# One trunk layer on one core: the first two input projections in two halves of the features, and the order of the first weight loads

## The reference

```python
sh1, sc1, g1, sh2, sc2, g2 = split(silu(cond) @ w_ada + b_ada, 6)   # "modulation", 12 blocks of 512 columns
h = ln_plain(x) * (1 + sc1) + sh1                                   # 384 x 1024
q_a, k_a, v_a, q_g, k_g, v_g, r_g, lr, mg = split(h @ w_in, ...)    # "projections"
attn = block_attention(rope(rms(q_a)), rope(rms(k_a)), v_a)
z = lr @ gla_w_gate + gla_b_gate ; logg = log_sigmoid(z) / 16
gla = rms(gla_scan(q_g, k_g, v_g, logg)) * silu(r_g)
merged = sigmoid(mg0) * (attn @ w_br_attn) + sigmoid(mg1) * (gla @ w_br_gla)
x = ln_affine(alpha * x + g1 * (merged @ w_out))
x = ln_affine(alpha * x + g2 * moe(ln_plain(x) * (1 + sc2) + sh2))  # top 2 of 32 experts
```

## Time and profile before

| | |
|---|---|
| median of three runs | 716.77 us |
| the profiled execution | 715.41 us, span 713.7 us |
| TensorE busy | 635.1 us, 89% of the span |
| VectorE, ScalarE, GpSimd busy | 277.9, 109.6, 113.1 us |
| HBM read | 174.55 MB |
| mean granted clock of TensorE | 0.941 |

### The profile page before, as it was taken

The page is one execution under the profiler, slowest core; times in us unless marked ns, Lnnn a source line. Parts: engine busy times, 40 slices in busy tenths (PEclk is TensorE's granted clock), DMA queues, the critical chain, the costliest instruction groups (busy, mean ns, idle before and its releaser), DMA issues.

```text
span 713.7 us, 8198 instructions
## 1 busy us (share of the span) xinstructions
PE 635.1 (89%) x3225; PEld 346.4 (49%) x3225; DVE 277.9 (39%) x568; ACT 109.6 (15%) x227; POOL 113.1 (16%) x115
## 2 busy tenths in 40 slices
PE   2899999999999999999999974899998888888894
PEld 0374345554444455556444453566664544544431
DVE  2421543236745445213224766133333222322247
ACT  0020252220012122215010020211111001100000
POOL 3000000020300000000000221433333222231100
PEclk9679999999999999999999985799999999999998
DMA  9977444236430230308968087599999999999852
GB/s 337 368 247 252 161 182 149 87 118 236 141 119 5 113 118 1 118 3 298 370 246 321 29 296 292 190 406 405 406 405 405 407 404 403 400 403 402 353 214 88
DMA packets 67495, 176.60 MB, mean 247 GB/s; under 512 B 10420, under 2 KB 12500, under 8 KB 67456
## 3 DMA queue, kind: packets, MB, share of 16 engines
q1 hardware_dynamic: 50832, 143.56, 52.8%
q10 hardware_dynamic: 10880, 24.21, 9.6%
q0 software_dynamic: 5744, 8.28, 3.3%
HBM read 174.55 MB, written 11.96 MB: 261 GB/s over the span
## 4 chain that ended last, share of the span: by engine, by line
PE 69%; DMA 15%; DVE 6%; SPq 6%; issue 2%; ACT 1%; POOL 1%; DVEq 0%; POOLq 0%
PE bank L1478 24%; PE bank L1733 10%; DMA X<-exp_w_up 9%; PE bank L1650 6%; PE bank L1664 6%; PE bank L1742 5%; DMA W<-exp_w_up 3%; DMA X<-w_ada 3%; SPq L451 3%; PE bank L1430 2%; PE bank L1608 2%; PE bank L1626 2%; PE bank L1531 1%; PE bank L1719 1%; SPq L461 1%
## 5 line engine op out<-in xcount | busy, mean ns | idle before, releaser
L1478 PE MATMUL bank<-W,Y 128*128 128x512 f32 (+1 forms) x432 | 183.0, 577 | 0.0
L1478 PEld LDWEIGHTS bank<-W,Y 128*128 128x128 f32 x432 | 80.9, 192 | 85.2 <-issue 82.6
L1733 PE MATMUL bank<-X,Y 128*64 128x256 f32 x704 | 86.6, 401 | 11.0 <-DMA X<-exp_w_up 10.2
L1733 PEld LDWEIGHTS bank<-X,Y 128*64 128x64 f32 x704 | 55.7, 145 | 48.0 <-DMA X<-exp_w_up 19.3
L630 POOL TENSOR_TENSOR rstd<-ss,cst 128x1 f32<-128x1 f32 (+3 forms) x21 | 22.6, 1074 | 339.2 <-DVE ss L760 339.2
L673 POOL DMA_INDIRECT Y<-h_rows,gidx x32 | 41.4, 1293 | 105.4 <-PE bank L1719 93.9
L1139 DVE COPY abias<-bank 128x128 f32<-128x128 f32 x32 | 9.3, 291 | 122.0 <-PE bank L1764 122.0
L1733 PE MATMUL bank<-W,Y 128*64 128x256 f32 (+1 forms) x320 | 39.7, 368 | 9.0 <-DMA W<-exp_w_up 4.6
L1742 PE MATMUL bank<-X,abias 128*64 128x512 f32 x176 | 42.6, 602 | 1.8 <-issue 1.8
L678 POOL DMA_INDIRECT pair_rows<-PTr,sidx x32 | 32.5, 1014 | 65.8 <-DVE PTr L1153 59.3
L1650 PE MATMUL bank<-W,Y 128*128 128x512 f32 x96 | 42.0, 594 | 0.3 <-PE bank L1650 0.3
(11 more groups left out here) (224 smaller groups left out, 705.6 us busy)
## 6 DMA issues: line engine op xcount, KB each, us to landing
X<-exp_w_gate SPq DMA_DIRECT2D x22, 1024.0 KB
X<-exp_w_up SPq DMA_DIRECT2D x22, 1024.0 KB
X<-exp_w_down SPq DMA_DIRECT2D x22, 1024.0 KB, 19.2
W<-w_in SPq DMA_DIRECT2D x8, 2048.0 KB, 9.0
Y<-w_ada ACTq DMA_DIRECT2D x8, 2048.0 KB, 9.2
W<-exp_w_gate SPq DMA_DIRECT2D x10, 1024.0 KB
W<-exp_w_up SPq DMA_DIRECT2D x5, 1024.0 KB
W<-exp_w_down SPq DMA_DIRECT2D x5, 1024.0 KB
```

The lines of the kernel that those rows point to most:

```text
L1478: ins = mm(bank[:, 0:cols], hT[:, i, k, :], w[:, k, :], start=k == 0, stop=k == KT - 1)
L1733: ins = mm(bank[hh * 64:hh * 64 + 64, a:b], x_[:, c, h * 64:h * 64 + 64], rhs(hh), start=k == 0 and a == 0, stop=k == KT - 1, skip_group_c ...
```

## The change

`WEIGHTS` loses ("ada", 1). SyncE's queue loads in the order: constants, x, block 0, block 2, the first half (features 0 to 511) of kvl, the first half of gqk, block 1, block 3, the second halves, the small tensors. Block 3 goes to `adabuf`. x is transposed and copied to `hT` by ScalarE as it is; VectorE then scales and shifts `hT` in place, half by half (`modulate(g)`). The two halved projections run their slices 0 to 3 first, for all tiles, and slices 4 to 7 later into the same banks. TensorE starts with 8 products on the constants that nobody reads (`keep_busy`). The step list moves: blocks 4 to 8 now stand behind projections 5 to 9 instead of 1, 3, 5, 7, 9; `lr` 1, `z` 1, `lr` 2 and `z` 2 go one or two projections later.

```diff
-AFTER[4] += [("z", 0), ("lr", 1), ("kprep", 1)]
-AFTER[5] += [("z", 1), ("lr", 2), ("kprep", 2)]
-AFTER[6] += [("kT", 0), ("kT", 1), ("z", 2), ("cum", 0)]
-AFTER[7] += [("kT", 2), ("kT", 3), ("tr", 0), ("cum", 1)]
+AFTER[4] += [("z", 0), ("kprep", 1)]
+AFTER[5] += [("lr", 1), ("kprep", 2)]
+AFTER[6] += [("z", 1), ("lr", 2), ("kT", 0), ("kT", 1), ("cum", 0)]
+AFTER[7] += [("z", 2), ("kT", 2), ("kT", 3), ("tr", 0), ("cum", 1)]
...
-for _n, _j in zip(range(4, 12), (1, 3, 5, 7, 9, 11, 12, 14)):
+for _n, _j in zip(range(4, 12), (5, 6, 7, 8, 9, 11, 12, 14)):
     AFTER[_j + 1].insert(0, ("rows", _n))
     AFTER[_j].insert(0, ("ada", _n))
...
+            def modulate(g):
+                bank = side.wait_full(dve, "modc", g)
+                mc = bank[:, 0:4 * KT].rearrange("p (k s) -> p k s", s=2)
+                ks = slice(4 * g, 4 * g + 4)
+                step(V.tensor_copy(modc[:, ks, :], mc[:, ks, :]))
+                ks = slice(KT + 4 * g, KT + 4 * g + 4)
+                ins = V.tensor_scalar_add(modc[:, ks, :], mc[:, ks, :], 1.0)
+                ...
+                for i in range(TILES):
+                    side.wait_read(dve, "xT", i, g)
+                    for k in range(4 * g, 4 * g + 4):
+                        ins = V.tensor_scalar(hT[:, i, k, :], hT[:, i, k, :], modc[:, KT + k, stream(i):stream(i) + 1],
+                                              modc[:, k, stream(i):stream(i) + 1], ALU.mult, ALU.add)
+                    ins.then_inc(h_ready[g], 1)
+            normed(0)
+            normed(1)
+            modulation(0)
+            normed(2)
+            modulation(2)
+            modulate(0)
+            modulation(1)
+            modulation(3)
+            modulate(1)
...
+            def x_columns(i):                                  # ScalarE
+                for g in range(2):
+                    bank = side.wait_full(act, "xT", i, g)
+                    side.was_read(A_(hT[:, i, 4 * g:4 * g + 4, :].rearrange("p k t -> p (k t)"), bank[:, :], ACT.Copy),
+                                  "xT", i, g)
+            x_columns(0)
+            x_columns(1)
+            main.wait_read(act, "ada", 0)
+            bias_rows(2)
+            x_columns(2)
+            main.wait_read(act, "ada", 1)
+            bias_rows(3)
+            main.wait_read(act, "ada", 2)
+            bias_rows(4)
+            main.wait_full(act, "ada", 3)
             ada_block(4)
...
+            def keep_busy(count):                              # TensorE
+                for _ in range(count):
+                    mm(banks[6][:, :], ident, cst[:, 0:HALF], start=True, stop=True)
...
             pe.wait_ge(S["consts_in"], 16)
+            keep_busy(FILL_START)                              # 8
+            x_transposes(0)
             pe.wait_ge(S["cond_silu"], 2)
+            modulation(0)
+            x_transposes(1)
+            columns(colbank, 0, 0)
+            x_transposes(2)
+            modulation(2)
+            side.filled(columns(colbank, 16, 2), "modc", 0)
+            for i in range(TILES):
+                project_half("kvl", i, 0)
+            modulation(1)
+            project_half("gqk", 0, 0)
+            columns(colbank, 8, 1)
+            modulation(3)
+            project_half("gqk", 1, 0)
+            side.filled(columns(colbank, 24, 3), "modc", 1)
+            project_half("gqk", 2, 0)
```

More of the change, by code:

```diff
@@ L96, in constants @@
     return c
-WEIGHTS = ([("ada", n) for n in range(2)]
+WEIGHTS = ([("ada", 0)]
            + [(x, 0) for x in ("kvl", "gqk", "vg", "q", "rg")] + [("mg", n) for n in range(4)]
@@ L147, with __init__ @@
 STEPS = [x for j in range(len(PROJ)) for x in AFTER[j]]
+FILL_START = 8
 class Banks:
-    def __init__(self, banks, full, read, jobs):
-        self.at = {}
-        uses = {b: 0 for b in range(len(banks))}
+    def __init__(self, ring, banks, full, read, jobs, uses, known=None):
+        self.at = dict(known or {})
         for n, job in enumerate(jobs):
-            b = n % len(banks)
+            b = ring[n % len(ring)]
             self.at[job] = (banks[b], full[b], read[b], uses[b])
@@ L185, in wait_read, with first_jobs @@
         eng.wait_ge(self.at[job][2], self.at[job][3] + 1)
+HALVED = ("kvl", "gqk")
+def first_jobs():
+    jobs = {("modc", g): 7 for g in range(2)}
+    jobs.update({("xT", 0, 0): 0, ("xT", 0, 1): 1, ("xT", 1, 0): 3, ("xT", 1, 1): 0, ("xT", 2, 0): 1, ("xT", 2, 1): 3})
+    jobs.update({("ada", n): 2 for n in (0, 2, 1, 3)})
+    for kind, ring in zip(HALVED, ((4, 5, 6), (0, 1, 3))):
+        jobs.update({("proj", kind, 0, i): ring[i] for i in range(TILES)})
+    return jobs
 def side_jobs():
-    jobs = [("modc", 0), ("xT", 0, 0), ("xT", 0, 1)] + [("xT", i, g) for i in (1, 2) for g in range(2)]
+    jobs = []
     for kind, a in STEPS:
@@ L211, in main_jobs @@
 def main_jobs():
-    jobs = [("ada", n) for n in range(4)]
+    jobs = []
     for j, x in enumerate(PROJ):
-        jobs += [("proj",) + x] + [step for step in AFTER[j] if step[0] == "ada"]
+        jobs += [("proj",) + x for _ in range(x[0] not in HALVED)] + [step for step in AFTER[j] if step[0] == "ada"]
     jobs += [("br", n, i, m) for n in range(2) for i in range(TILES) for m in range(2)]
@@ L405, in program @@
         read = [sem(f"bank{i}_read") for i in range(8)]
-        main = Banks(banks[0:2], full[0:2], read[0:2], main_jobs())
-        side = Banks([banks[i] for i in (2, 3, 7)], [full[i] for i in (2, 3, 7)],
-                     [read[i] for i in (2, 3, 7)], side_jobs())
+        uses = [0] * 8
+        first = Banks(list(first_jobs().values()), banks, full, read, list(first_jobs()), uses)
+        main = Banks((0, 1), banks, full, read, main_jobs(), uses, first.at)
+        side = Banks((2, 7, 3), banks, full, read, side_jobs(), uses, first.at)
         outb = [banks[4], banks[5], banks[6]]
@@ L1236, in _ @@
             A_(conde[:, :, :], cond[:, :, :], ACT.Exp, scale=-1.0).then_inc(S["cond_exp"], 1)
[L1237 to L1242, removed]
-            ada_block(4)
[L1244 to L1251, removed]
+            def x_columns(i):
[13 more added lines that the diff above has]
+            main.wait_full(act, "ada", 3)
+            ada_block(4)
+            main.wait_read(act, "ada", 3)
+            bias_rows(5)
             exps = [0]
@@ L1432, in modulation @@
                 main.filled(ins, "ada", n)
-                if n < 2:
+                if n == 0:
                     main.wait_full(pe, "ada", n)
@@ new lines, in project_half @@
+            def project_half(kind, i, g):
+                if g == 0:
+                    pe.wait_ge(half_in[kind], 32 if kind == "kvl" else 16)
+                    bank = main.claim(pe, "proj", kind, 0, i)
+                else:
+                    weights(kind, 0)
+                    bank = main.bank("proj", kind, 0, i)
+                pe.wait_ge(h_ready[g], i + 1)
+                cols = KVL if kind == "kvl" else HALF
+                w = W[:, WJ[kind, 0] % 2, 0:KT * cols].rearrange("p (k n) -> p k n", k=KT)
+                for k in range(4 * g, 4 * g + 4):
+                    ins = mm(bank[:, 0:cols], hT[:, i, k, :], w[:, k, :], start=k == 0, stop=k == KT - 1)
+                if g:
+                    main.filled(ins, "proj", kind, 0, i)
+                    if i == TILES - 1:
+                        main.wait_full(pe, "proj", kind, 0, i)
+                        used(pe.nop(), kind, 0)
```

114 lines of the change are left out of this document (52 added, 62 removed).

## The result

The changed kernel takes 729.9 us (median of 4 runs, 727.76 to 730.47) against 715.9 us on the same chip: ratio 1.0194, 95% interval 1.0167 to 1.022, so 14 us slower. The forecast was 727, range 714 to 736. The profiled execution took 730.36 us, span 728.6: 14.9 us more span than before.

What follows compares the result with a forecast made beforehand. It took TensorE in program order as the bound behind the start, and loads plus TensorE's lower clock within it. Start -12.9, step lists +22.6, clock +1.0 made +10.7 us on 715.4, 726; the median 727, range 714 to 736.

Steps and rivals of the forecast that it cites:

- T: End of the last gqk projection, 84.9 us before: forecast at 72.0, 12.9 earlier.
- the fill: The products at TensorE's start that nobody reads: end at 14.5 us, as block 0 lands, so cost nothing in the middle case.
- The bias row of block 2: Start, small load on ScalarE's queue: charged nothing; if served first come, first served, T would be 8 us later.
- the way I had written down: Start: lower clock from TensorE's 2 us idle stretch ending at 21.5 us; half projections start at 31.1 against 43.5.
- waits on blocks 5 to 8: Between T and Q: late requests make TensorE wait 3.2, 2.2, 2.0 and 2.0 us, 9.4 in all.
- idle stretches in lists 6 and 7: Step lists with blocks 5 and 6: TensorE idles 3.7 and 4.5 us, behind z's round trip.
- the clock behind T: Idle stretches of about 4 us may lower TensorE's clock: 0 to 2.8 us for each of three lists, 1.0 taken.
- ScalarE's lag: From a block's start to ScalarE's request for the next: 11.6 us behind block 5, 13.3 behind block 6.
- Q: Start of the second q projection, 143.5 us before: T + 81.2 against T + 58.6; its shift should stand at the end.
- The blocks are in time: Rival, blocks behind T: no round trip shows, Q at 136.5, kernel at 710 us (706 with a warm start); chance 0.15.
- Warm start, shorter lists: Rival: T at 67.8, a microsecond less for each of lists 5 to 8, +2.5 us in all, 719; chance 0.13.
- Cold lists: Rival: clock falls in every gap, fill runs cold, T at 76, 2 us for each of three lists: 736; chance 0.12.

Runs made afterwards that it cites:

- experiment 6: The changed kernel without the 8 products at the start that nobody reads: 732.22 us, ratio 1.0253 to the kernel before.
- Experiment 8: Changed kernel with z and lr in their old lists, other banks, ScalarE asking first, blocks 4 to 8 behind projections 1, 4, 6, 7, 9: 711.05 us, ratio 0.9948.
- Experiment 1: The changed kernel with ScalarE asking for the next block ahead of its other work in the list: 723.65 us, ratio 1.011 to the kernel before.
- experiment 4: The kernel before with only the changed kernel's step list: 737.17 us, ratio 1.0272 to the kernel before.
- 9: The kernel of Experiment 8 with five more products that nobody reads in the start's idle stretches: 706.89 us, ratio 0.9905 to the kernel before.
- experiment 5: The changed kernel with products that nobody reads in TensorE's idle stretches behind the last gqk projection: 727.87 us, ratio 1.0183 to the kernel before.
- 3: The changed start with the whole step list of the kernel before, five results in other banks: 715.98 us, ratio 1.0012 to the kernel before.
- 7: The changed kernel with SyncE loading blocks 1 and 3 ahead of the first halves of kvl and gqk: 733.90 us, ratio 1.0285 to the kernel before.
- 2: The changed kernel with lr 1, z 1, lr 2 and z 2 each back by one list: 725.27 us, ratio 1.0126 to the kernel before.

## Why the prediction was right

**The start.** T was forecast at 72.0 and came at 70.9. Block 0 landed at 14.6 in experiment 6, where TensorE waited for it (forecast 14.5), and the fill took 9.55 us, to 14.4, forecast 14.5. The bias row of block 2, charged at nothing, cost nothing: it was asked for at 18.45, and VectorE's add at 24.34 waited for TensorE alone. The clock took another way to nearly the same end: it held through block 2, so the half projections began at 27.9 instead of 31.1, and it fell at 26 to 28, so the first halves of kvl took 8.94 us instead of 6.9. Two misses, 3.2 us less and 2.0 more, nearly cancel in T, and that part is luck. Experiment 8 shows the way I had written down (falling at 20 to 22, start at 31.0).

**The blocks.** This was the step on which the sign hung, and it held in each place: waits on blocks 5 to 8 of 4.1, 1.95, 1.95 and 1.7 us (forecast 3.2, 2.2, 2.0, 2.0), idle stretches in lists 6 and 7 of 3.7 and 4.5 us (0.55 + 3.19 and 0.51 + 4.03; forecast 3.7 and 4.5), a load in 8.6 to 11.0 us. Experiment 1 shows that for blocks 6 to 8 the request and not the transfer was late, experiment 4 that the list alone does it.

**The term that was mis-sized.** I priced the clock behind T at 1.0 us. Against the same instructions in the trace of before, block 5 took 1.2 us more, its rows 0.6, cum 0 with its last products 2.1; block 6 1.0, its rows 0.8, cum 1 1.1: 6.8 us in all, and T to Q was 87.9 instead of 81.2, 6.7 more. As the products of cum end ScalarE's lag, the lags grew to 14.8 and 15.9 (forecast 11.6 and 13.3). My bound, up to 2.8 us in each of three lists, counted only the products of a cum. It was passed in list 6 (3.9) and just in list 7 (2.9), because a block and its rows, right behind the wait on the block, ran at the lower clock too; list 8 cost nothing. Only the bound of all three together, 8.4, held, and my choice of 1.0 in it was too low. The rest of the difference is small: Q +15.2 against +10.7, the span +14.9, the median +14.

**The rivals.** "The blocks are in time" fell with the four waits. A list in which they are in time is seen in experiments 8 and 9, though there z and lr have moved back too. "Warm start, shorter lists" (719) was right on the clock up to the first half projection (27.9, its start being 27.6), but T was 70.9 and not 67.8, lists 5 to 7 were longer than forecast, and list 8 was shorter by 0.7 us only (18.7 from block 7 to block 8, forecast 19.4). "Cold lists" (736) was right in mechanism for two of three lists, but without the cold fill.

**Open.** How much the clock behind T costs in the median: profile and runs differ in experiment 5. Why the clock falls at 20 us in one execution and at 26 in another of the same start isn't settled. Experiment 8 changes the request, the places of z and lr and the spacing at once, and no run has the first two without the third, so their shares in its gain aren't known.

## What to carry to other kernels

A load that a compute engine asks for comes as late as that engine's place in its own program: count from the event that frees the buffer to the request, add the landing time, and compare with the work between two uses. When steps are moved to make room for a better start, price the list they are moved into: here 6 to 8 us were won ahead of T, and some 20 were lost behind it. The two can be had together, as experiments 8 and 9 show, once the blocks are spaced by what a request plus a landing takes, the request comes first in its list, and the round trips are back where they were.

## What the runs showed of the hardware

- The same start held TensorE's clock until 24 to 26 us in four profiles (changed, 1, 3 and 7), where block 2 took 1.92 us, and lost it at 20 to 22 us in three (2, 5 and 8), where it took 3.57 to 3.64. It fell each time in a stretch of light work with idle gaps of 0.9 to 2.1 us. The half projections started at 27.3 to 27.9 in the changed kernel, 1 and 3, and at 31.0 in 8, but were slower behind the later fall: the first halves of kvl were done at 36.7 in the changed kernel and at 38.7 in 8, so 2 us of the 3 were left. Five more products in the gaps held the clock in the one profile taken with them.
- The record of the granted clock starts at 1.00, and it read so from 10 to 18 us in the kernel before, while the 16 instructions of block 0 took 3.64 us, the lower clock's time. In the changed kernel, behind the fill, they took 1.93 at the same reading. In the first microseconds the durations tell the clock, not the column.
- VectorE's multiply and add in place on 128 elements in SBUF took 3.16 / 12 = 0.26 us, against 1.37 / 4 = 0.34 from PSUM.
